# Means over the features of a transformer kernel: GpSimd adds the tiles, TensorE multiplies twice; two MLPs without engine meetings

## What is computed

```python
# first block, twice: mixer m, then
h = layer_norm(ALPHA * x + m, ln1_g, ln1_b)
f = square(relu(h @ mlp_w1)) @ mlp_w2             # 1024 -> 4096 -> 1024
e = sigmoid(h @ ple_w_gate) * (p @ ple_w_proj)
x = layer_norm(ALPHA * h + f + e, ln2_g, ln2_b)
# layer_norm: mu = mean(x), var = mean((x - mu)**2), over the 1024 features
# second block, twice: y = mixer(modulate(x, ..)); mod from c @ ada_w
x = x + mod[2] * y
x = x + mod[5] * mlp(modulate(x, norm2_g, mod, 3))
# modulate: x * rsqrt(mean(x * x) + eps) * g * (1 + scale) + shift
```

## Time and profile before

| | before |
|---|---|
| median of three runs | 3378.65 us |
| the profiled execution, its own time | 3379.38 us |
| its span, first to last instruction | 3377.6 us |
| PE busy | 3189.2 us (94%) |
| DVE busy | 1586.0 us (47%) |
| ACT busy | 1220.4 us (36%) |
| POOL busy | 78.8 us (2%) |
| mean granted clock of PE | 0.968 of full |

### The profile page before, as it was taken

How to read it: one execution, slowest core, us unless ns; L and a number is a source line. 1 busy time by engine, 2 the same in 40 slices (tenths; PEclk the granted TensorE clock), 3 DMA queues, 4 the chain that set the end, 5 groups by cost and what they waited for, 6 DMA issues and landing times. The chain is left out here.

```text
span 3377.6 us, 39289 instructions
## 1 busy us (share of the span) xinstructions
PE 3189.2 (94%) x15148; PEld 2490.1 (74%) x15148; DVE 1586.0 (47%) x2389; ACT 1220.4 (36%) x2029; POOL 78.8 (2%) x84
## 2 busy tenths in 40 slices
PE   7989999999898999998998998999999997999999
PEld 5666677763486677775885786788888784778887
DVE  4863666661154466665424633433333424334444
ACT  2543233322463333335213453422222324543332
POOL 2200000000000000000001100000000000000000
PEclk9969999999998999999998998999999999999999
DMA  5101443422301343340211000121212120022221
GB/s 185 51 25 38 174 165 122 172 103 33 92 1 50 115 159 145 141 162 20 63 50 50 1 1 26 50 75 50 75 50 75 50 75 1 1 75 100 89 85 74
DMA packets 157676, 259.15 MB, mean 77 GB/s; under 512 B 54332, under 2 KB 70074, under 8 KB 157436
## 3 DMA queue, kind: packets, MB, share of 16 engines
q1 hardware_dynamic: 155812, 252.66, 21.3%
q10 hardware_dynamic: 1628, 4.76, 0.4%
q0 software_dynamic: 128, 0.26, 0.0%
HBM read 255.57 MB, written 2.10 MB: 76 GB/s over the span
## 5 line engine op out<-in xcount | busy, mean ns | idle before, releaser
L1195 ACT ACTIVATE w_hi<-wbuf 128x1024 fp32r<-128x1024 f32 x330 | 348.4, 1058 | 1211.6 <-PE psA L751 1171.8
L749 PE MATMUL psA<-act_hi,w_hi 128*128 128x512 f32 (+1 forms) x1824 | 694.8, 381 | 59.6 <-DVE act_lo L1821 32.0
L750 PE MATMUL psA<-act_lo,w_hi 128*128 128x512 f32 (+1 forms) x1824 | 682.9, 374 | 0.0
L751 PE MATMUL psA<-act_hi,w_lo 128*128 128x512 f32 (+1 forms) x1824 | 681.9, 374 | 0.0
L1815 DVE TENSOR_TENSOR w_lo<-wbuf,w_hi 128x1024 fp32r<-128x1024 f32 x330 | 404.9, 1230 | 542.0 <-ACT w_hi L1195 537.3
L749 PE MATMUL psA<-hid_hi,w_hi 128*128 128x512 f32 (+1 forms) x1280 | 476.4, 372 | 4.7 <-DVE work L1922 4.6
L750 PE MATMUL psA<-hid_lo,w_hi 128*128 128x512 f32 (+1 forms) x1280 | 471.9, 369 | 0.0
L751 PE MATMUL psA<-hid_hi,w_lo 128*128 128x512 f32 (+1 forms) x1280 | 471.6, 368 | 0.0
L749 PEld LDWEIGHTS psA<-act_hi,w_hi 128*128 128x128 f32 x1824 | 349.8, 192 | 132.1 <-issue 52.4
L750 PEld LDWEIGHTS psA<-act_lo,w_hi 128*128 128x128 f32 x1824 | 349.7, 192 | 62.0 <-issue 3.6
L751 PEld LDWEIGHTS psA<-act_hi,w_lo 128*128 128x128 f32 x1824 | 348.9, 191 | 61.0
(11 more groups left out here) (228 smaller groups left out, 3537.5 us busy)
## 6 DMA issues: line engine op xcount, KB each, us to landing
wbuf<-in_mlp_w_dram SPq DMA_DIRECT2D x64, 2048.0 KB, 8.4
work<-in_ada_w_dram SPq DMA_DIRECT2D x32, 1536.0 KB, 10.9
wbuf<-in_ab_w_in_dram SPq DMA_DIRECT2D x10, 1024.0 KB, 5.0
wbuf<-in_ple_w_gate_dram SPq DMA_DIRECT2D x4, 2048.0 KB, 7.5
wbuf<-in_hy_w_in_dram SPq DMA_DIRECT2D x3, 2048.0 KB, 13.6
wbuf<-in_c_w_in_dram SPq DMA_DIRECT2D x3, 2048.0 KB, 7.5
wbuf<-in_hy_w_out_dram SPq DMA_DIRECT2D x2, 2048.0 KB, 7.8
wbuf<-in_mla_w_out_dram SPq DMA_DIRECT2D x2, 2048.0 KB, 7.7
```

The lines of the kernel that those rows point to most:

```text
L749: pe.matmul(psA[:, s, a:b], w_hi, x_hi[:, a:b], start=first, stop=False)
L750: pe.matmul(psA[:, s, a:b], w_hi, x_lo[:, a:b], start=False, stop=False)
L751: ins = pe.matmul(psA[:, s, a:b], w_lo, x_hi[:, a:b], start=False, stop=last)
L1195: return nc.scalar.activation(out, in_, func, **kw)
```

## The change

POOL adds tiles 0 to 6 of each of the seven means (six adds each), as they become ready, into one tile. PE then multiplies `C["mean"]` with that sum and, when it is there, with tile 7: two matmuls in place of eight. PE no longer has the interleaved ones. `ln_m1` and `ln_m3` are gone as products; their means come right behind the MLP's last tile, in `psB[:, 1, :]`. DVE signals each final `acc` tile behind a drain. The four meetings round `mlp0` and `mlp1` are gone; ACT waits for `ple_set` of DVE before the MLP instead. Of the context squares for `rms0`, those of tiles 2 to 7 move on ACT behind the squares of layer norm 3.

```diff
+        out_sum = area(LAT, at=4 * KD * TOK + TOK)
...
+            def mean_of_tiles(stage, out, x, last_set):
+                pe.wait_ge(S["tile_sum"], SUMMED[stage] + 1)
+                total, n = tile_sums[stage], tile_sums[stage].shape[-1]
+                spans = ((0, 512), (512, n)) if n > 512 else ((0, n),)
+                for a, b in spans:
+                    pe.matmul(out[:, a:b], C["mean"], total[:, a:b], start=True, stop=False)
+                last_set(KD - 1)
+                return [pe.matmul(out[:, a:b], C["mean"], x[:, KD - 1, a:b], start=False, stop=True) for a, b in spans]
...
             def mean_of(stage):
 
                 def add(k):
-                    emptied(pe, stage, k)
-                    ins = pe.matmul(psO[:, 0:LAT], C["mean"], xT[:, k, 0:LAT], start=(k == 0), stop=(k == KD - 1))
                     if k == KD - 1:
-                        ins.then_inc(S["sum_ready"], 1)
+                        mean_of_tiles(stage, psO, xT, lambda k: emptied(pe, stage, k))[-1].then_inc(S["sum_ready"], 1)
                 return add
...
             def layer_norm(i, x):
-                if i % 2:
-                    product(f"ln_m{i}", 0, [(0, LAT, [(C["mean"], x[:, k, 0:LAT]) for k in range(KD)])])
                 sum_squares(f"ln_v{i}", ln_squares[i], LAT)
...
+                if name in ADA:
+                    mean_of_tiles(name, psB[:, 1, :], acc, lambda k: pe.wait_ge(S["acc_set"], KD * ADA[name] + k + 1))[-1].then_inc(
+                        S["acc_mean"], 1)
...
             ple(0)
-            meet(pe)
             mlp("mlp0", 0, LAT)
-            meet(pe)
             layer_norm(1, acc)
...
+                if name in ADA:
+                    act.wait_ge(S["ple_set"], ADA[name] + 1)
...
+            context_squares(range(2))
+            layer_norm(3, acc, "ln2_b", 8, xT, between=lambda: context_squares(range(2, KD)), behind=lambda k: f(
...
+            def sum_tiles(stage, x, tile_set):
+
+                total = tile_sums[stage]
+                n = total.shape[-1]
+                tile_set(0)
+                for k in range(1, KD - 1):
+                    tile_set(k)
+                    nc.gpsimd.tensor_tensor(total, x[:, 0, 0:n] if k == 1 else total, x[:, k, 0:n], ALU.add)
+                    pool.drain()
+                pool.drain().then_inc(S["tile_sum"], 1)
...
+            sum_tiles("hy_out", xT, lambda k: emptied(pool, "hy_out", k))
+            sum_tiles("mlp0", acc, lambda k: pool.wait_ge(S["acc_set"], k + 1))
...
             nc.gpsimd.memset(accs[TOK], 0.0).then_inc(S["acc_zero"], 1)
+            sum_tiles("ab_out", hraw, squared(1))
+            sum_tiles("mlp2", squares[TOK], squared(2))
...
             nc.gpsimd.memset(accs[LAT], 0.0).then_inc(S["acc_zero"], 1)
+            sum_tiles("c_out", hraw, squared(3))
...
+                v.drain().then_inc(S["ple_set"], 1)
                 w_lo(f"mlp{l}", 0)
...
                         tt(acc[:, j, :], acc[:, j, :], ps[:, 0:n], ALU.add).then_inc(free, 1)
+                        if last and name in ADA:
+                            v.drain().then_inc(S["acc_set"], 1)
```

More of the change, by code:

```diff
@@ L554, in build @@
         rms_squares = [4 * KD + KD * i for i in range(4)]
+        SUMMED = {n: i for i, n in enumerate(("hy_out", "mlp0", "mla_out", "mlp1", "ab_out", "mlp2", "c_out"))}
+        tile_sums = {**{n: out_sum for n in ("hy_out", "mla_out")}, **{n: pT[:, 0, 0, :] for n in ("mlp0", "mlp1")},
+                     **{n: flatP[:, 0:TOK] for n in ("ab_out", "mlp2")}, "c_out": flatP[:, 0:LAT]}
         def turned_groups(name, qt):
@@ L940, in rms @@
             def rms(i, n):
-                sum_squares(f"rms{i}", rms_squares[i], n)
+                if i == 0:
+                    sum_squares(f"rms{i}", rms_squares[i], n)
+                else:
+                    s, c = A("rms2", 0)
+                    pe.wait_ge(a_free[s], c)
+                    mean_of_tiles("mlp2", psA[:, s], squares[n], lambda k: pe.wait_ge(S["squared"], rms_squares[i] + k + 1))[-1].then_inc(
+                        a_ready[s], 1)
             def mlp(name, index, n):
@@ L1293, in inverse_root, with layer_norm @@
                 f(dst, dst, ACT.Exp, scale=-0.5).then_inc(free, 1)
-            def layer_norm(i, x, bias, j0, dst, x_hi=None, ahead=(), behind=None):
+            def layer_norm(i, x, bias, j0, dst, x_hi=None, ahead=(), behind=None, between=None):
                 for a in ahead:
@@ L1499, in _, with context_squares @@
             ple(1)
[L1500 removed]
             mlp("mlp1", 1, LAT)
[L1502 to L1505 removed]
+            def context_squares(ks):
+                act.wait_ge(S["acc_mean"], 2)
+                for k in ks:
+                    f(squares[TOK][:, k, LAT:TOK], xT[:, k, LAT:TOK], ACT.Square)
+            context_squares(range(2))
+            layer_norm(3, acc, "ln2_b", 8, xT, between=lambda: context_squares(range(2, KD)), behind=lambda k: f(
                 squares[TOK][:, k, 0:LAT], xT[:, k, 0:LAT], ACT.Square).then_inc(S["squared"], 1))
@@ L1677, in _, with squared @@
             meet(pool)
-            for _ in range(PRE_LSTM):
-                meet(pool)
+            def sum_tiles(stage, x, tile_set):
[7 more added lines that the diff above has]
+                pool.drain().then_inc(S["tile_sum"], 1)
+            def squared(i):
+                return lambda k: pool.wait_ge(S["squared"], rms_squares[i] + k + 1)
+            meet(pool)
+            sum_tiles("hy_out", xT, lambda k: emptied(pool, "hy_out", k))
+            sum_tiles("mlp0", acc, lambda k: pool.wait_ge(S["acc_set"], k + 1))
+            meet(pool)
+            sum_tiles("mla_out", xT, lambda k: emptied(pool, "mla_out", k))
+            sum_tiles("mlp1", acc, lambda k: pool.wait_ge(S["acc_set"], KD + k + 1))
+            meet(pool)
+            meet(pool)
             nc.gpsimd.memset(win_mask, 0.0)
```

39 lines of the change are left out of this document (13 added, 26 removed).

## The result

Four runs of the changed kernel took 3337.03 us in the median (3334.86 to 3342.27), four of the kernel before (the three given ahead of the prediction and one more) 3378.98 us: a ratio of 0.9881 (95% interval 0.9869 to 0.9893), 41.9 us less. Three more comparisons, with other executions of both kernels, stand further down and gave 0.9884, 0.9877 and 0.9886. The forecast was 3339 us, within 3329 to 3354.

A forecast was written before the change was run, and what follows sets the result against it. The prediction took PE as the bound inside the products and all engines as one chain at a mean. Savings of 10.4 + 6.4 + 4.5 + 5.1 + 10.0 + 2.8 = 39.2 us from 3378.65 gave 3339 us, range 3329 to 3354.

The forecast's parts named there:

- The tile's price: In the projections, each interleaved tile of a mean costs PE 0.90 us at 512 tokens and 1.28 us at 768.
- layer norms 0 and 2: Means behind `hy_out` and `mla_out`: five interleaved tiles removed, 4.5 us, plus 0.7 us at the end; 10.4 us for both.
- rms1: Mean in `ab_out`, 768 tokens: five interleaved tiles removed from PE, 6.4 us saved, nothing at the end.
- rms3: Mean in `c_out`: five interleaved tiles of 0.90 us removed from PE, 4.5 us saved, nothing at the end.
- The tails worth nothing: Ends of `ab_out` and `c_out`: ACT reaches the root from its own `w_hi`, so PE finishing sooner saves nothing.
- Ends of `mlp0` and `mlp1`: Layer norms 1 and 3: 6.0 us saved each, less 1.0 for DVE's drains and POOL's work in the last group; 10.0 together.
- The slack of 0.3 us: Last group of `mlp0`: about 0.3 us of DVE delay is absorbed before PE waits; PE waits for what exceeds it.
- rms2: Mean behind `mlp2`: 5.35 us saved, bounded by ACT's two `w_hi`, less 0.25 for POOL slowing DVE's add; 5.1 us.
- Starts: Starts of `mlp0` and `mlp1`: PE waits only for the first `w_lo`, not the meeting; 1.4 us each, 2.8 together.
- Contention: Rival: POOL's adds slow DVE and DVE slows PE at the MLP ends; 11 us back, 3350 us, chance 0.12.
- POOL too slow: Rival: PE waits for POOL's sum at the MLP ends; at 5 us per add 3388 us, chance 0.04.
- The clock: Rival: each of nine PE restarts after pauses costs 3.4 us more at half clock; 15 us lost, 3355 us, chance 0.09.

## Why the prediction was right, and where it was off

The forecast of 3339 us missed the median by 2 us, but two errors of opposite sign stand behind that: the places gave 2.5 us less than forecast, and 5.2 us came from outside them. Some 3 us of these go with the lower half-clock time of the changed kernel, which the forecast didn't have; the rest is the chance of this comparison (the three others gave 40.0, 40.2 and 39.2 us where this one gave 41.9). That the total came so close is luck in that part.

- **The tile's price** held. Every projection unit came to 5.44 us, the 768-column ones lost 1.30 us (1.28 forecast); layer norms 0 and 2 gave 10.3 for 10.4, rms1 6.5 for 6.4, rms3 4.5.
- **The tails worth nothing** held: the roots of rms1 and rms3 come from ACT's `w_hi`, as the row without a bracket had said.
- **Ends of `mlp0` and `mlp1`.** Gross 6.1 us for 6.0. The charge in the last group was 1.45 us each for 1.0: chosen too near the low end, since the mean over all `w_lo` says nothing of the few that meet an addition. The one row of 2.37 us was the right witness. The slack of 0.3 us was read right: most of the two us of held time reached PE.
- **rms2** is the step that failed: 5.1 us forecast, 2.9 measured. It allowed 0.25 us for DVE beside POOL, as if the addition of tile 7 were the only one to meet POOL; but that one reads PSUM and was at 0.94 us. The instructions that were held are the residuals, the last three by 1.6 us each, which delayed ACT's `w_hi` by 1.6 us; the forecast kept the squares at their old times, at which the two wouldn't have met, and so missed that the first hold moves the additions onto the residuals. PE idled 3.40 us before the sum, where 1.3 was expected. A further 0.84 us went to PE's sum at half clock. Without the sixth addition the place gave 5.5 us.
- **Starts**: 3.2 us for 2.8, the price of a meeting there. The half-clock stretch stayed behind the start of `mlp0`, as forecast.
- **Contention** as a rival was right in kind and too large in price: 11 us more in the forecast's terms, 0.9 + 1.3 measured. In the last group it is mainly two of the additions that cost, those ahead of PE's two pauses; PE's slack takes most of the others (moving one of them brought 0.2 us), and additions that meet reads of PSUM are free. The forecast took it as a slowing down, a little for each; the rows show the one waiting for the other's whole instruction, and only for some kinds of instruction. The Trainium skill states just that on another page than the one I had weighed ("SBUF — State Buffer", section "SBUF: two separate sides": the port pair that VectorE and GpSimd share is an exclusive lock, whoever starts first has it for the whole instruction, and a VectorE instruction takes part when it has two SBUF inputs and GpSimd reads SBUF). By that rule, which the rows shown here bear out, a residual of 1.15 us that meets an addition of 1.84 had to be charged with all that is left of the addition.
- **POOL too slow** didn't come up: an addition of 512 columns took 1.28 us and of 768 columns 1.84, for 1.34 and 2.0 estimated. The doubled additions show how near `mlp2` is to it: twice the work cost 7.6 us there.
- **The clock** went the other way from the rival: half-clock time fell, over all executions from 210.5 to 199.3 us, and gave about 3 us, 5 in the profiles. In the forecast it stood with one sign only, and at nothing in the sum. A kernel whose pauses and matmuls are rearranged can gain as well as lose there.

## What to carry to other kernels

Work given to POOL was free where DVE at that moment read PSUM or waited, or where nobody waited for what DVE was held at: for each addition look at which DVE instruction it will meet (with two SBUF inputs it waits until the addition is done, 1.22 us becoming 2.23), what that shifts, and who waits for it, not at DVE's busy share or at the mean of a group. Let the last tile or two go straight to PE, since the helper's last step sits on the path. And when an edit is worth a few us out of thousands, judge it by its places in two traces: the 16 executions of one program lay between 3333.2 and 3342.3 us, and the longer ones were those with more time at half clock.

## What was not expected of the hardware

Of the first point I had expected the kind and not the size:

- A DVE instruction with two inputs in SBUF and an addition on POOL didn't run at once: `w_lo` 1.22 us alone and 2.23 beside one, the residual 1.15 and 2.74, a pair of tiny additions 0.33 and 1.24; POOL's own addition goes from 1.28 to 2.27 us. An addition of DVE with one input in PSUM kept its 0.69 us.
- The same program had 192.3, 196.5, 199.3 and 206.1 us at half clock in four profiles; one stage with the same matmuls took 319.6 or 322.7 us.
- A short pause ahead of a small product can cost twice: PE idled 3.40 us for POOL's sum and then took 2.90 us for four matmuls that take 1.45 at full clock.
